# Score jobs ahead of the transposes in each attention item

## The reference

```
ss    = einsum(qb, kg)                    # scores of the selected blocks
ps    = masked_softmax(ss, pos <= t)
o_slc = einsum(ps, vg)
pwin  = masked_softmax(einsum(qb, kwb), mw)
o_win = einsum(pwin, vwb)
pc    = masked_softmax(einsum(qb, kc), mc)     # 31 compressed blocks
o_cmp = einsum(pc, vc)
out   = gate0 * o_cmp + gate1 * o_slc + gate2 * o_win
```

## Time and profile before

| what | value |
|---|---|
| median of 3 runs | 1377.58 us (1377.1 to 1378.83) |
| profiled execution | 1377.06 us |
| its span on the core | 1375.3 us |
| PE busy | 1348.6 us, 98% |
| DVE, ACT, POOL busy | 724.6, 603.6, 699.0 us |
| attention items, layer 0 | about 200.8 to 298 us |
| attention items, layer 1 | about 678 us later |

### The profile page before, as it was taken

How to read it: one execution, slowest core, us unless ns; L and a number is a source line. 1 busy time by engine, 2 the same in 40 slices (tenths; PEclk the granted TensorE clock), 3 DMA queues, 4 the chain that set the end, 5 groups by cost and what they waited for, 6 DMA issues and landing times.

```text
span 1375.3 us, 17665 instructions
## 1 busy us (share of the span) xinstructions
PE 1348.6 (98%) x6888; PEld 1111.4 (81%) x6888; DVE 724.6 (53%) x910; ACT 603.6 (44%) x1041; POOL 699.0 (51%) x544
## 2 busy tenths in 40 slices
PE   8999999999999999999999999999999999999998
PEld 5889876778888888888888888767798888888886
DVE  5406658745554544654463075677455554556443
ACT  5233577745433333423451335676463333334222
POOL 2644677744544444544454456776544444445441
PEclk9999999999999999999999999999999999999999
DMA  5433320031423332333133334101233332333331
GB/s 206 138 100 108 117 84 16 1 123 62 120 94 92 102 98 92 96 103 92 62 123 101 116 99 137 32 16 46 77 99 101 104 95 92 105 95 92 98 102 61
DMA packets 34882, 127.18 MB, mean 92 GB/s; under 512 B 3952, under 2 KB 4464, under 8 KB 34416
## 3 DMA queue, kind: packets, MB, share of 16 engines
q1 hardware_dynamic: 34656, 125.53, 29.4%
q10 hardware_dynamic: 144, 0.52, 0.1%
HBM read 123.94 MB, written 2.10 MB: 92 GB/s over the span
## 4 chain that ended last, share of the span: by engine, by line
PE 87%; ACT 5%; DVE 5%; issue 2%; POOL 1%; DMA 0%; DVEq 0%; POOLq 0%; ACTq 0%; SPq 0%
PE bank L1762 33%; PE bank L1412 18%; PE bank L1794 17%; PE bank L1428 5%; PE bank L1656 3%; PE bank L1694 1%; ACT E L826 1%; PE bank L1516 1%; DVE s_bias L1211 1%; DVE pt_l L946 1%; PE bank L1623 1%; PE bank L1721 1%; PE bank L1720 1%; PE bank L1380 1%; PE bank L1602 1%
## 5 line engine op out<-in xcount | busy, mean ns | idle before, releaser
L550 POOL TENSOR_TENSOR w_lo<-raw,w_hi 128x1024 fp32r<-128x1024 f32 x216 | 520.6, 2416 | 469.0 <-ACT w_hi L650 468.7
L650 ACT ACTIVATE w_hi<-raw 128x1024 fp32r<-128x1024 f32 x220 | 231.0, 1055 | 241.6 <-DMA raw<-wstream 241.5
L1762 PE MATMUL bank<-act_hi,w_hi 128*128 128x512 f32 (+1 forms) x768 | 286.0, 372 | 0.6 <-DVE act_lo L946 0.6
L1762 PE MATMUL bank<-act_lo,w_hi 128*128 128x512 f32 (+1 forms) x768 | 285.2, 371 | 0.0
L1762 PE MATMUL bank<-act_hi,w_lo 128*128 128x512 f32 (+1 forms) x768 | 285.2, 371 | 0.0
L905 ACT ACTIVATE cv<-bank,par 128x512 f32<-128x512 f32 x88 | 68.4, 778 | 286.0 <-PE bank L1762 286.0
L1341 DVE SCALAR_TENSOR_TENSOR cv<-bank,par,cv 128x511 f32<-128x511 f32 x88 | 66.0, 750 | 225.2 <-ACT cv L905 225.2
L1762 PEld LDWEIGHTS bank<-act_hi,w_hi 128*128 128x128 f32 x768 | 144.6, 188 | 26.9 <-DVE act_lo L946 1.6
L1762 PEld LDWEIGHTS bank<-act_lo,w_hi 128*128 128x128 f32 x768 | 144.7, 188 | 25.0
L1762 PEld LDWEIGHTS bank<-act_hi,w_lo 128*128 128x128 f32 x768 | 144.7, 188 | 24.9
L1412 PE MATMUL bank<-w_hi,act_hi 128*128 128x512 f32 (+1 forms) x384 | 144.5, 376 | 0.6 <-DVE w_lo L946 0.5
(11 more groups left out here) (177 smaller groups left out, 2172.6 us busy)
## 6 DMA issues: line engine op xcount, KB each, us to landing
raw<-wstream SPq DMA_DIRECT2D x220, 512.0 KB, 3.6
g_all<-gains SPq DMA_DIRECT2D x2, 2048.0 KB, 7.2
x_out<-x SPq DMA_DIRECT2D x8, 256.0 KB, 2.0
x<-x_in SPq DMA_DIRECT2D x3, 512.0 KB, 9.2
const<-consts SPq DMA_DIRECT2D x1, 1030.0 KB, 13.8
g_all<-gains ACTq DMA_DIRECT2D x1, 512.0 KB, 5.4
x<-x_in SPq DMA_DIRECT2D x2, 256.0 KB, 5.4
par<-pars SPq DMA_DIRECT2D x2, 235.0 KB, 3.7
```

Of the source, the lines that this page charges most:

```text
L550: nc.gpsimd.tensor_tensor(w_lo[:, s, :], raw_slot(s), r32(w_hi[:, s, :]), ALU.subtract)\
L650: nc.scalar.activation(w_hi[:, s, :], raw_slot(s), ACT.Copy).then_inc(hi_ready, 1)
L1762: last = mm(bank[:, b, first:end], a, v, start=(k == 0 and n == 0), stop=(k == KD - 1 and n == 2), skip_group_check=True)
```

## The change

In each item PE sends the item's score jobs first, and then the transposes and the product, where it sent them behind the product. Fillers stay behind. No instruction is added, removed or altered; the other engines' queues are as they were, and so are all semaphore counts.

```diff
                 for k in range(NI):
+                    for z in jobs_at(k):
+                        job_scores(z)
                     turn_p(k)
                     if k >= 2:
                         product(k - 2)
-                    for z in jobs_at(k):
-                        job_scores(z)
                     if k in Q7_AT:
                         if k == min(Q7_AT):
                             pe.wait_ge(c_step, upto(c_step, l, 3))
```

## The result

The changed kernel takes 1385.97 us (median of 4 runs, 1384.85 to 1386.18) against 1377.34 us (4 runs, 1376.63 to 1378.83): ratio 1.0059, 95% interval 1.0047 to 1.0071. It is slower by 8.6 us. The forecast was 1385.4 us, range 1378 to 1389.5.

The account below looks back on a forecast made before the run. TensorE, busy 98% of the span, was taken as the bound. Lateness of 3.9 us a layer, +7.8 over two layers, on the profiled 1377.06 gives 1384.9; with the median 0.5 above it, 1385.4 us, range 1378 to 1389.5.

Parts of the forecast that it names:

- Gaps filled, effect 1: Jobs come 0.35 + 0.55 us earlier and fill gaps where transposes waited for VectorE; gain at most the gap.
- Product and copy later, effect 2: Transposes and product come one job later, 1.07 or 0.6 us; ScalarE's copy and its followers too, where no backlog.
- copy(7): ScalarE's high-half copy in item 7: to move from 215.50 to 216.57; staying at 215.5 would prove the prediction wrong.
- The bank's wait ahead of T, effect 3: A job's wait for its bank's earlier exp now precedes transposes and product; cover falls from 3.0 to 1.5 us.
- all five places: Items 19, 27, 29, 31 and 39: new waits of jobs for ScalarE's exp, 4 us a layer.
- S(29): Score job sent in item 29: to start at 261.91; a start before 261 would prove the prediction wrong.
- The chain handed on through VectorE and ScalarE: From item 7, ScalarE's and VectorE's backlog runs 1.1 us late and stays so, making later transposes wait.
- Sum: Lateness after item 39 of 3.9 us a layer stays to the end; two layers, +7.8 us.
- weight load passed a waiting job: Assumed not to happen; if it did, five waits a layer give back some 0.1 us each, total +6.8.
- that nothing waits: Rival: gaps are filled and exps are ready; 2.4 us a layer come back, 1372.8 us; chance 0.06.
- that only direct waits count: Rival: copies don't shift; waits at items 27, 29, 39 cost 2.0 a layer, gaps return 2.4; 1376.8; chance 0.14.
- the ring of banks: Rival: three banks become the bound, 0.2 us waits in ten of items 16 to 28; 1389.4 us; chance 0.10.

Follow-up runs that it names:

- item 7 alone: Score jobs sent ahead of the transposes in item 7 only, against the kernel before: 1380.93 us against 1377.53, ratio 1.0024.
- the early items: Score jobs sent ahead of the transposes only in items 3 to 26, against the kernel before: 1379.9 us against 1377.53, ratio 1.002.
- the run without item 7: The full change except in item 7, against the kernel before: 1382.71 us against 1377.53, ratio 1.0037.
- the repeat: The changed kernel run once more, one run, beside the kernel before: 1384.88 us against 1377.49.
- the late items: Score jobs sent ahead of the transposes only in items 27 to 39, against the kernel before: 1383.17 us against 1377.53, ratio 1.0041.
- the jobs between: Score jobs sent between the transposes and the product in all items, against the kernel before: 1389.23 us against 1377.49, ratio 1.0082.
- the filler with job 30: Kernel before with item 27's output-projection filler ahead of the transposes and item 29's job sent in item 30: 1377.81 us against 1377.6, ratio 1.0004.
- both edits: Kernel before with item 27's filler first, item 29's job in item 30, and two weight chunks later: 1376.01 us against 1377.6, ratio 0.9986.
- the quiet items: The change in all items but 7, 19, 27, 29, 31, 37 and 39, against the kernel before: 1378.92 us against 1377.49, ratio 1.001.
- the two fillers: Kernel before with the output-projection fillers of items 27 and 47 ahead of the transposes: 1378.85 us against 1377.49, ratio 1.0007.
- the weight chunks: Kernel before with the output projection's second and third weight chunks handled later on ScalarE and GpSimd: 1375.89 us against 1377.6, ratio 0.9988.

## Why the prediction was right

By its steps. **Gaps filled, effect 1:** seen, but worth little: where the clock stayed up, the transposes' waits fell by 0.4 us a layer, since new waits came at T(11) and T(38) (0.47 and 0.78 us in the change) for those that went at T(27) and T(37). **Product and copy later, effect 2:** seen at copy(7), and isolated by the run of item 7 alone, where PE does the same work, no job waits, and each layer still ends 1.1 us late or more. **The bank's wait ahead of T, effect 3:** seen at all five places, at times 0.1 us ahead of the forecast once the 0.2 us offset is added (S(29) forecast at 261.91, measured at 261.59 + 0.21; S(31) 264.88 and 264.77; S(39) 281.3 and 281.2). The waits sum to 3.6 us a layer, where 4 were forecast. **The chain handed on through VectorE and ScalarE:** shown by the early items, which make T(27) late by 1.13 us (expected 1.1) with PE's own order there untouched. **Sum:** 7.8 us forecast, 7.5 measured in the items. The median rose by 8.6 us, so 1.1 us of it lie outside the items and were not forecast; that the median came within 0.6 us of the number is in that part luck.

Mis-sized was the division of the total. The prediction had PE 0.7 us late after item 23; in the run without item 7 I took all of that for its chain and expected the rest to cost 3.2 us a layer. Measured, item 7 is worth 1.1 us, and the rest without it 2.65. In the full change the sum came out since errors of 0.4 and 0.5 go against each other. The ledger of the run without item 7 (layer 0) says where: PE is 0.4 us ahead after item 23, not on time, since the gaps filled in items 10 to 18 keep something; from there the steps are 0.55 to item 27, 1.3 to 31 and 1.2 to 39 (expected 0.6, 1.5 and 1.1).

No weight load passed a waiting job. PE's weight loads at S(27) and T(27) in the changed kernel, layer 0:

```profile
254.97 0.10 PEld L1597 LDWEIGHTS bank<-causal_b,ident_b 128*128 128x128 bf16 x1 [1.98 <-ACT E L826]
...
255.28 0.54 PEld L1694 LDWEIGHTS bank<-const,E 128*128 128x128 f32 x4
```

The loads stood idle for 1.98 us until the exp was done, and the first load of T(27) came 0.31 us behind that of the job. The transposes kept their distance, T(27) starting 0.48 us after S(27) (254.98 to 255.46) and T(29) 0.60 after S(29), as long as the jobs themselves are. The Trainium skill ("TensorE: Matmul & The Clock Gate", Architectural detail) speaks of loads pulled ahead of matmuls in flight; past a job that waits for a semaphore these rows show none.

The rivals: that nothing waits is refuted by the five waits; that only direct waits count, by the early items and by item 7 alone; the ring of banks did not become a bound of its own: of the jobs' four waits for L826 in PE's list none is in items 20 to 26, where jobs follow each other.

## What to carry to other kernels

In an in-order queue a filler should stand behind what the slower engines are waiting for, and ahead of what waits for them. Moving it ahead of both fills a gap once and delays the release of the next round each time; if it has a wait of its own, that wait is handed to all behind it. To shorten a gap, ask first which queue is late and take something out of that queue in that stretch: moving two weight copies on ScalarE brought 1.7 us here (0.4 to 2.9), while two re-orderings of PE's fillers brought nothing.

## What the runs showed of the hardware that I had not expected

**The clock can fall after the gap at item 10.** Windows of the changed kernel, layer 0; the last three columns are granted clock, DMA share and GB/s:

```profile
220.00:222.00 2.00, 0.83 (x5) 0.60 (x5) 1.11 (x3) 1.94 (x4) 0.00 (x0) 1.00 0.00 0
222.00:223.00 1.00, 0.53 (x3) 0.28 (x3) 1.00 (x2) 0.60 (x1) 0.00 (x0) 0.73 0.00 0
223.00:224.00 1.00, 1.00 (x5) 0.97 (x5) 1.00 (x3) 0.00 (x0) 0.66 (x1) 0.50 0.08 16
...
225.00:226.00 1.00, 1.00 (x6) 0.88 (x5) 0.97 (x3) 0.51 (x2) 0.90 (x3) 0.56 0.00 0
```

PE was busy 0.83 of the 2 us from 220 to 222, and the granted clock went to 0.50 (1.2 of 2.4 GHz) until shortly before 226. T(11) took 1.11 us in place of 0.62. Before, the same gap was there (1.63 us) and the clock stayed at 1.00. Over the profiles it fell at items 10 to 13 in both layers of the repeat, of the early items and of item 7 alone, and in one layer of the change, the late items, the jobs between, the filler with job 30, and both edits; it did not in the kernel before, all but item 7, the quiet items, the two fillers, and the weight chunks. The late items' run has the order of before at items 10 to 13 and shows it in layer 1, so it isn't bound to the change. It is more frequent with the job of item 7 ahead of its transposes: in 7 of 8 layers (the change, its repeat, the early items, item 7 alone), against 4 of the 18 layers of the other nine kernels. Its price is mostly hidden: in layer 0 of the change T(12) is 2.6 us late and T(14) 1.0, since T(14) waits for VectorE anyway, as late as in layer 1, where the clock stayed. Where something was left over it was 0.2 to 1.2 us a layer. What decides whether it falls was not tried.

**VectorE held up by GpSimd.** In layer 1 of the first profile a VectorE operation on 128x24 elements took 2.27 us beside a GpSimd split; its twin before took 0.16. There are four such operations a layer. After, then GpSimd, then two of them before:

```profile
800.60 0.16 DVE L1050 TENSOR_SCALAR gate<-gate 128x24 f32<-128x24 f32 x1
...
801.02 2.27 DVE L1050 TENSOR_SCALAR gate<-gate 128x24 f32<-128x24 f32 x1
```

```profile
800.90 2.35 POOL L550 TENSOR_TENSOR w_lo<-raw,w_hi 128x1024 fp32r<-128x1024 f32 x1 [0.99 <-ACT w_hi L650]
```

```profile
793.89 1.77 DVE L1050 TENSOR_SCALAR gate<-gate 128x24 f32<-128x24 f32 x1
...
796.74 0.16 DVE L1050 TENSOR_SCALAR gate<-gate 128x24 f32<-128x24 f32 x1
```

It ended 0.04 us after the split did (803.29 and 803.25), and PE waited 1.54 us for it. Such a hold-up is in every trace: the first of the four takes 1.76 to 1.79 us in both layers of all 13, the kernel before included, beside a split that began 0.65 us ahead of it, and ends 0.03 to 0.04 us behind that split. The order matters: in the early items' run the last of the four began 0.09 us ahead of a split and took its usual time.

```profile
798.10 0.17 DVE L1050 TENSOR_SCALAR gate<-gate 128x24 f32<-128x24 f32 x1
```

```profile
798.19 2.37 POOL L550 TENSOR_TENSOR w_lo<-raw,w_hi 128x1024 fp32r<-128x1024 f32 x1 [1.20 <-ACT w_hi L650]
```

The Trainium skill ("SBUF — State Buffer", SBUF: two separate sides) says that the pair of ports that VectorE and GpSimd share is an exclusive lock: of a GpSimd operation and a VectorE operation that needs the pair (in a two-port mode, or with two inputs in SBUF), the one that starts first has it for the whole instruction. The rows agree; which mode this operation ran in they do not show. The change does not cause the second hold-up: in the repeat the four operations of that layer are as before, one slow and three at 0.16 us. It accounts for about 1.5 us of the first profile's 9.1.
